# Row factors of three norms sent to all partitions through a DRAM scratch instead of through TensorE

## Chip, cores and metric

The kernel runs on one core of a Trainium2 chip. The metric is the device time of one execution in microseconds, as the median of several; lower is better.

## What is computed

A sequence of 256 tokens with 1024 features passes through four residual blocks, and nearly all of the work is matrix products in fp32 quality. Cut to what matters here:

```python
def rmsnorm(x, g):                                   # also rms_norm of the second part
    y = x * lax.rsqrt(jnp.mean(x * x, axis=-1, keepdims=True) + 1e-6)
    return y * g

# first part, two layers
h = h + attention(rmsnorm(h, norm_mix[0]))           # norm L0
h = h + sq_relu_mlp(rmsnorm(h, norm_mlp[0]))         # norm M0
h = h + rglru_block(rmsnorm(h, norm_mix[1]))         # norm L1
h = h + sq_relu_mlp(rmsnorm(h, norm_mlp[1]))         # norm M1
h = rmsnorm(h, norm_final)
# second part, one layer
h = h + 0.5 * swiglu(rms_norm(h, ffn1_norm), gate, up, down)   # norm F1
h = h + mixer(rms_norm(h, mix_norm))                           # norm X2
h = h + 0.5 * swiglu(rms_norm(h, ffn2_norm), gate, up, down)   # norm F2
out = rms_norm(h, final_norm)

def swiglu(x, w_gate, w_up, w_down):
    return (jax.nn.silu(x @ w_gate) * (x @ w_up)) @ w_down
```

A norm divides each token (row) by a factor of its own. That division commutes with a product over the features, so the kernel multiplies the un-normed rows by the weights and applies the factor afterwards.

## The kernel before, in words

**Pieces.** All weights stream through SBUF as 167 pieces of 1 MB, each of 128 partitions by 2048 fp32. SyncE loads a piece into one of four `raw` buffers as soon as `lo_done` says that an earlier one is free. ScalarE (`hi`) rounds it to `w_hi`, VectorE (`lo`) subtracts to get `w_lo`, and TensorE multiplies with both halves, so that three products stand for one fp32 product. ScalarE and VectorE stay three pieces ahead of TensorE (`LOOK`). Every engine runs its own program in written order, and semaphores tie them together.

**A SwiGLU block** (`feed_forward` for `F1` and `F2`) goes over 11 pairs of column blocks. For each pair TensorE multiplies a gate piece and an up piece (`u_piece` with `u_wide`), and a down piece of the pair before (`d_piece`). The results of the up products have the features on the partitions and the tokens along the free axis. So the row factor, which is one number per token, is needed as a row of 256 numbers that is the same on all 128 partitions: the tile `rms`. For pair 0 VectorE runs `gate` (times `rms`), ScalarE the Silu, then VectorE and ScalarE make `z`, `z_hi` and `z_lo` (`z_finish`), and the first `d_piece` of TensorE waits for both (`z_ready`). The sums `tmp[0]` and `tmp[1]` have left PSUM before that, so nothing but this chain needs `rms`.

**The attention block** (`L0`) needs `rms` when `qk_leave` copies the query and key products out of PSUM. Its position bias is made on GpSimd's queue: a table goes to a DRAM scratch (`er_dram`), comes back by a 2 MB transfer into `bias`, and a memset closes it (`bias_done`).

**How `rms` is made before.** The factors exist as `rstd`, with a token on each partition (128 partitions by 2). GpSimd computes it in `rstds` (a power of -0.5). VectorE's `diags(j)` multiplies the identity by each of the two columns. TensorE's `spread(j)` multiplies a matrix of ones by the two diagonals into a PSUM bank, and VectorE's `spread(j)` copies that bank into `rms`. This stands at five norms (`SPREAD`: L0, L1, F1, X2, F2). At F1 the factor is the product of two norms' factors: `both_rstds()` multiplies `rstd` by `rstd2` on VectorE after the split of piece `n0 + 4` and signals `rstd_both`. TensorE's `spread(F1)` comes after product 7 of the second gate piece, and `spread(F2)` after product 4 of its own; `spread(L0)` stands right ahead of the query and key pieces.

**GpSimd's queue** also issues the small constant loads: after `hn_rstd` of F1 the rope table, `mats`, the mask and `pool_m`; after `rstds(F2)` the last norm's gain.

## Time and profile before

| | |
|---|---|
| median of 3 runs | 1013.86 us (1012.96 to 1013.97) |
| the profiled execution | 1013.26 us |
| its span, first to last instruction | 1011.5 us |
| TensorE busy | 1003.2 us, 99% |
| VectorE, ScalarE, GpSimd busy | 68%, 55%, 3% |
| granted TensorE clock, mean | 0.999 |
| HBM read and written | 183.14 MB and 1.07 MB |

The time of an execution is 1.8 us more than its span, and the profiled execution lies 0.6 us below the median. Busy times of TensorE are modelled for a pipelined engine, so that what a matmul costs is the distance from its start to the next start, and not its own duration.

### The profile page before, as it was taken

What the parts mean: (1) busy time and instruction counts of PE and PEld (TensorE: products, weight loads), DVE (VectorE), ACT (ScalarE), POOL (GpSimd) and SP (SyncE); (2) the same over time, 40 slices, a digit from 0 to 9 for tenths busy, and PEclk for the clock granted to TensorE, in tenths of its full rate; (3) what the DMA queues carried; (4) which work ended last, traced back from release to release, by engine and by line L of the source; (5) the groups of instructions that cost most, each with busy time, mean ns of one, the idle gap of its engine ahead of it and who ended that gap; (6) DMA issues with size and microseconds to landing.
All of it is one profiled execution on the core that took longest, in us unless ns stands there. A gap on an engine that the chain in (4) does not pass through costs nothing.

```text
span 1011.5 us, 14177 instructions
## 1 busy us (share of the span) xinstructions
PE 1003.2 (99%) x5632; PEld 857.4 (85%) x5632; DVE 684.5 (68%) x925; ACT 556.8 (55%) x807; POOL 35.0 (3%) x38
## 2 busy tenths in 40 slices
PE   9999999999999999999999999999999999999997
PEld 7988788888889988888888888888888788888886
DVE  6777676666667887666566766656578767666564
ACT  6678654444456866443444645545457655545453
POOL 1000010000002300000000200000010010000000
PEclk9999999999999999999999999999999999999999
DMA  9943385564553445745655566565633365665621
GB/s 339 324 133 126 125 280 176 200 208 167 188 187 126 167 167 193 245 167 199 212 173 171 207 198 226 190 208 167 208 114 107 115 204 172 228 208 167 208 84 42
DMA packets 122287, 185.13 MB, mean 183 GB/s; under 512 B 3130, under 2 KB 100590, under 8 KB 122094
## 3 DMA queue, kind: packets, MB, share of 16 engines
q1 hardware_dynamic: 119952, 176.70, 52.4%
q0 software_dynamic: 1808, 6.93, 1.9%
q8 instruction: 45, 0.74, 0.3%
q10 hardware_dynamic: 462, 0.60, 0.2%
q14 instruction: 20, 0.16, 0.0%
HBM read 183.14 MB, written 1.07 MB: 182 GB/s over the span
## 4 chain that ended last, share of the span: by engine, by line
PE 96%; DVE 2%; ACT 1%; DMA 1%; issue 1%; SPq 0%
PE bank L1493 37%; PE bank L1470 28%; PE bank L1472 14%; PE bank L1456 3%; PE bank L1458 3%; PE bank L1459 3%; PE bank L1519 1%; DVE w_lo L784 1%; PE bank L1614 1%; PE bank L1665 1%; PE bank L1642 1%; PE bank L1626 1%; DMA raw<-in_w_qkv 1%; PE bank L1810 0%; PE bank L1811 0%
## 5 line engine op out<-in xcount | busy, mean ns | idle before, releaser
L784 DVE TENSOR_TENSOR w_lo<-raw,w_hi 128x2048 fp32r<-128x2048 f32 x164 | 374.0, 2289 | 130.5 <-ACT w_hi L386 130.5
L1470 PE MATMUL bank<-xT,w_hi 128*128 128x512 f32 x1216 | 431.4, 398 | 0.0
L1472 PE MATMUL bank<-xT,w_lo 128*128 128x256 f32 x1216 | 341.1, 280 | 0.0
L386 ACT ACTIVATE w_hi<-raw 128x2048 fp32r<-128x2048 f32 x164 | 311.7, 1908 | 37.5 <-PE bank L1493 33.5
L1470 PEld LDWEIGHTS bank<-xT,w_hi 128*128 128x128 f32 x1216 | 228.4, 188 | 55.7 <-issue 0.3
L1472 PEld LDWEIGHTS bank<-xT,w_lo 128*128 128x128 f32 x1216 | 229.6, 189 | 1.9
L1493 PE MATMUL bank<-w_hi,z_hi 128*128 128x512 f32 x472 | 153.9, 394 | 0.2
L1493 PE MATMUL bank<-w_lo,z_hi 128*128 128x512 f32 x472 | 152.3, 391 | 0.0
L1493 PE MATMUL bank<-w_hi,z_lo 128*128 128x512 f32 x472 | 151.7, 390 | 0.0
L429 ACT ACTIVATE work<-bank 128x256 f32<-128x256 f32 x152 | 49.8, 379 | 178.8 <-PE bank L1472 178.8
L859 DVE TENSOR_TENSOR work<-bank,work 128x256 f32<-128x256 f32 x152 | 57.1, 418 | 74.0 <-ACT work L429 74.0
L1493 PEld LDWEIGHTS bank<-w_lo,z_hi 128*128 128x128 f32 x472 | 88.6, 188 | 19.3 <-issue 0.2
L1493 PEld LDWEIGHTS bank<-w_hi,z_lo 128*128 128x128 f32 x472 | 88.6, 188 | 19.3
L1493 PEld LDWEIGHTS bank<-w_hi,z_hi 128*128 128x128 f32 x472 | 85.0, 188 | 18.5 <-issue 1.3
L1456 PE MATMUL bank<-xT,w_hi 128*128 128x256 f32 x304 | 89.9, 296 | 0.0
L444 ACT ACTIVATE z_hi<-work 128x512 fp32r<-128x512 f32 x54 | 34.1, 632 | 99.7 <-DVE work L876 53.0
L1458 PE MATMUL bank<-xT,w_hi 128*128 128x256 f32 x304 | 85.9, 282 | 0.0
L1459 PE MATMUL bank<-xT,w_lo 128*128 128x256 f32 x304 | 85.8, 282 | 0.0
L887 DVE TENSOR_TENSOR z_lo<-work,z_hi 128x512 fp32r<-128x512 f32 x54 | 37.4, 692 | 37.7 <-ACT z_hi L444 37.7
L1456 PEld LDWEIGHTS bank<-xT,w_hi 128*128 128x128 f32 x304 | 58.0, 191 | 2.4 <-issue 1.2
L1458 PEld LDWEIGHTS bank<-xT,w_hi 128*128 128x128 f32 x304 | 58.1, 191 | 0.3
L1459 PEld LDWEIGHTS bank<-xT,w_lo 128*128 128x128 f32 x304 | 58.1, 191 | 0.0
(215 smaller groups left out, 775.5 us busy)
## 6 DMA issues: line engine op xcount, KB each, us to landing
raw<-in_w SPq DMA_DIRECT2D x64, 1024.0 KB, 5.3
raw<-in_f_gate SPq DMA_DIRECT2D x22, 1024.0 KB, 5.3
raw<-in_f_up SPq DMA_DIRECT2D x22, 1024.0 KB, 5.8
raw<-in_f_down SPq DMA_DIRECT2D x22, 1024.0 KB, 4.9
raw<-in_w_in SPq DMA_DIRECT2D x13, 1024.0 KB, 5.4
raw<-in_w_qkv SPq DMA_DIRECT2D x9, 1024.0 KB, 8.6
raw<-in_w_o SPq DMA_DIRECT2D x4, 1024.0 KB, 5.0
raw<-in_rec_w_o SPq DMA_DIRECT2D x4, 1024.0 KB, 5.2
```

Of the source, the lines that this page charges most:

```text
L386: e.activation(w_hi[n % RING], raw[n % RAW], ACT.Copy).then_inc(hi_done, 1)
L429: e.activation(low[:, b * S:(b + 1) * S], bank[n][:, S:2 * S], ACT.Copy).then_inc(z_low, 1)
L444: e.activation(z_hi[:, s, :], tmp[f.nu], ACT.Copy).then_inc(zhi_done, 1)
L784: e.tensor_tensor(w_lo[n % RING], raw[n % RAW], r32(w_hi[n % RING]), ALU.subtract).then_inc(lo_done, 1)
L859: e.tensor_tensor(t[:, here], bank[n][:, 0:S], low[:, here], ALU.add).then_inc(z_sum, 1)
L887: e.tensor_tensor(z_lo[:, s, :], z, r32(z_hi[:, s, :]), ALU.subtract).then_inc(zlo_done, 1)
L1456: e.matmul(o, whi[:, k, cut], xT_hi[:, k, :], start=(k == 0 and b == 0), stop=False, skip_group_check=True)
L1458: e.matmul(o, whi[:, k, cut], xT_lo[:, k, :], start=False, stop=False, skip_group_check=True)
L1459: last = e.matmul(o, wlo[:, k, cut], xT_hi[:, k, :], start=False, stop=(k == KB - 1), skip_group_check=True)
L1470: e.matmul(bank[i], whi[:, k, cut], xT[:, k, :, :].rearrange("p b s -> p (b s)"), start=(k == 0), stop=False, skip_group_check=True)
L1472: last = e.matmul(bank[i][:, 0:S], wlo[:, k, cut], xT_hi[:, k, :], start=False, stop=(k == KB - 1), skip_group_check=True)
L1493: mm = e.matmul(acc[t][half], x, w[:, kk, half * 512:(half + 1) * 512], start=(first and kk == 0 and x is xhi and w is whi), stop=(last an ...
```

## The change

`SPREAD` now holds only L1 and X2. At L0, F1 and F2 the diagonals, the matmuls by ones and the copy from PSUM are gone. In their place GpSimd writes `rstd` to a DRAM scratch `rms_dram` as a row of 256 numbers (`factors_out`), waits until that has landed, and reads the row back into `rms` on all 128 partitions (`factors_in`). What used to wait for `rms_done` at these norms now waits for `rms_in`.

```diff
-SPREAD = {j: i + 1 for i, j in enumerate((L0, L1, F1, X2, F2))}
+NORMED = {j: i + 1 for i, j in enumerate((L0, L1, F1, X2, F2))}
+SPREAD = {L1: 1, X2: 2}
...
@@ vector(e) @@
         def diags(j):
-            if j == F1:
-                e.wait_ge(rstd_both, 1)
-            else:
-                e.wait_ge(rstd_done, SPREAD[j])
+            e.wait_ge(rstd_done, NORMED[j])
...
-            if j in SPREAD and j != F1:
+            if j in SPREAD:
                 diags(j)
...
@@ gate(f, p) @@
             else:
-                e.wait_ge(rms_done, SPREAD[f.j])
+                e.wait_ge(rms_in[f.j], 16)
             e.tensor_tensor(pair(tmp[0]), pair(tmp[0]), rms_pair(), ALU.mult).then_inc(z_g, 1)
...
                 if f.j == F1:
                     both_rstds()
-                    diags(F1)
...
-                spread(f.j)
+                if f.j == F1:
+                    e.wait_ge(rstd_both, 1)
+                else:
+                    e.wait_ge(rstd_done, NORMED[f.j])
                 e.tensor_scalar(down_scale, rstd, 0.5, None, ALU.mult).then_inc(scale_done, 1)
                 gate(f, 0)
...
         variance(L0)
-        diags(L0)
...
         lo(5)
-        spread(L0)
         lo(6)
-        e.wait_ge(rms_done, SPREAD[L0])
+        e.wait_ge(rms_in[L0], 16)
         qk_leave(0)
...
@@ gpsimd(e) @@
+        def factors_out(j):
+            e.dma_start(rms_dram[NORMED[j] - 1, :].rearrange("(t p) -> p t", p=P), rstd,
+                        allow_slow_non_contiguous=True).then_inc(rms_out[j], 16)
+
+        def factors_in(j):
+            e.wait_ge(rms_out[j], 16)
+            e.dma_start(rms, row_bcast(rms_dram[NORMED[j] - 1, :], S)).then_inc(rms_in[j], 16)
...
         rstds(L0)
+        e.wait_ge(rstd_done, NORMED[L0])
+        factors_out(L0)
+        factors_in(L0)
         e.wait_ge(er_out, 16)
         e.dma_start(bias, bass.AP(tensor=er_dram.tensor, offset=0, ap=[[1, P], [ER, N_HEADS], [1, S]])).then_inc(
             in_bias, 16)
...
         e.tensor_tensor(rstd2, var, minus_half, ALU.pow).then_inc(hn_rstd, 1)
+        e.wait_ge(rstd_both, 1)
+        factors_out(F1)
+        factors_in(F1)
         e.dma_start(cs_t, A["rope"]).then_inc(in_rope, 16)
...
         rstds(F2)
+        e.wait_ge(rstd_done, NORMED[F2])
+        factors_out(F2)
+        factors_in(F2)
         e.dma_start(nf, row_bcast(A["norm_last"], D)).then_inc(in_norm_last, 16)
...
@@ tensor(e) @@
-                ups(p, {7 if f.j == F1 else 4: lambda: spread(f.j)} if p == 1 and f.nu == 2 else None)
+                ups(p)
...
-        spread(L0)
...
-        e.wait_ge(rms_done, SPREAD[L0])
         e.wait_ge(bias_done, 1)
```

Line numbers of the changed kernel run higher than those of before: `w_lo` of a piece is L784 before and L787 now, a matmul of the up products L1470 and L1472 before and L1487 and L1489 now, one of the down products L1493 and L1510.

On GpSimd, at the attention norm L0, the queue stood so before; the first row is the factor, `work<-er_scratch` is the 2 MB load of the bias, and the memset closes the bias.

```order
L1397 DMA er_scratch<-work 16x384 [waits er_far,er_near]
L1385 TENSOR_TENSOR rstd<-var,minus_half 128x2 [waits var_done,consts]
L1401 DMA work<-er_scratch 128x16x256 [waits er_out]
L1404 MEMSET work 64x16x64 [waits in_bias]
L1406 DMA gate_w<-in_w_ga 128x8x128 [waits var_done]
```

Now it stands so.

```order
L1405 DMA er_scratch<-work 16x384 [waits er_far,er_near]
L1385 TENSOR_TENSOR rstd<-var,minus_half 128x2 [waits var_done,consts]
L1388 DMA rms_scratch<-rstd 128x2x1 [waits rstd_done]
L1393 DMA rms<-rms_scratch 128x256 [waits rms_out0]
L1412 DMA work<-er_scratch 128x16x256 [waits er_out]
L1415 MEMSET work 64x16x64 [waits in_bias]
```

Two transfers have moved in ahead of the bias load, and the second of them waits for the landing of the first.

On GpSimd at F1 and F2 the queue now reads as follows; without the four rows that name `rms_scratch` it is the order of before.

```order
L1446 TENSOR_TENSOR rstd<-var,minus_half 128x2 [waits hn_var]
L1388 DMA rms_scratch<-rstd 128x2x1 [waits rstd_both]
L1393 DMA rms<-rms_scratch 128x256 [waits rms_out4]
L1450 DMA work<-in_rope 128x512
L1451 DMA work<-in_mats 128x640
L1452 DMA work<-in_mask 128x512
L1453 DMA work<-in_pool_m 128x2048
L1385 TENSOR_TENSOR rstd<-var,minus_half 128x2 [waits var_done] x2
L1388 DMA rms_scratch<-rstd 128x2x1 [waits rstd_done]
L1393 DMA rms<-rms_scratch 128x256 [waits rms_out6]
L1459 DMA work<-in_norm_last 128x1024
```

The constant loads of F1 now stand behind the pair of transfers, and so does the gain of the last norm.

On VectorE at F1 the rows from the product of the two factors to the first `z_lo` were these before.

```order
L784 TENSOR_TENSOR w_lo<-raw,w_hi 128x2048 [waits hi_done,z_sum]
L905 TENSOR_TENSOR rstd<-rstd 128x2 [waits hn_done,hn_rstd]
L828 TENSOR_SCALAR diag<-ident,rstd 128x128 [waits rstd_both]
L828 TENSOR_SCALAR diag<-ident,rstd 128x128
L851 COPY rms<-bank 128x256 [waits spread_done]
L928 TENSOR_SCALAR down_scale<-rstd 128x2
L867 TENSOR_TENSOR work<-work,rms 128x512 [waits rms_done]
L884 TENSOR_TENSOR work<-work 128x512 [waits z_s]
L887 TENSOR_TENSOR z_lo<-work,z_hi 128x512 [waits z_f,zhi_done]
```

Now they are these.

```order
L787 TENSOR_TENSOR w_lo<-raw,w_hi 128x2048 [waits hi_done,z_sum]
L905 TENSOR_TENSOR rstd<-rstd 128x2 [waits hn_done,hn_rstd]
L930 TENSOR_SCALAR down_scale<-rstd 128x2 [waits rstd_both]
L867 TENSOR_TENSOR work<-work,rms 128x512 [waits rms_in4]
L884 TENSOR_TENSOR work<-work 128x512 [waits z_s]
L887 TENSOR_TENSOR z_lo<-work,z_hi 128x512 [waits z_f,zhi_done]
L787 TENSOR_TENSOR w_lo<-raw,w_hi 128x2048 [waits hi_done]
```

Three rows are gone, and the multiplication by `rms` (L867) waits for the second transfer in place of the copy.

## Rows read from the trace of the kernel before

**Rows 1.** The page: busy time, share of the span and instructions of each engine.

```profile
PE 1003.2 (99%) x5632; PEld 857.4 (85%) x5632; DVE 684.5 (68%) x925; ACT 556.8 (55%) x807; POOL 35.0 (3%) x38
```

**Rows 2.** The page: the chain that ended last, share of the span by engine.

```profile
PE 96%; DVE 2%; ACT 1%; DMA 1%; issue 1%; SPq 0%
```

**Rows 3.** Waits of TensorE: engine line waited for: us in total, times, longest.

```profile
PE bank L1650 <- POOL zeros L1387: 1.0, 1, 1.0
PE bank L1626 <- DVE work L990: 0.9, 2, 0.5
PE bank L1665 <- ACT w_hi L391: 0.2, 1, 0.2
...
PEld bank L1614 <- DVE z_lo L951: 0.4, 1, 0.4
```

**Rows 4.** One line, the matmuls by ones: count, ns min/median/max, first and last start.

```profile
L1561 PE MATMUL bank<-diag,ones x20: 270/275/377, 30.2 to 835.8; 128*128 128x128 f32 x20
```

**Rows 5.** TensorE in order of time at F1: start us, us, what.

```profile
576.77 0.67 PE L1561 MATMUL bank<-diag,ones 128*128 128x128 f32 x4
577.20 0.47 PE L1470 MATMUL bank<-xT,w_hi 128*128 128x512 f32 x1
577.51 0.27 PE L1472 MATMUL bank<-xT,w_lo 128*128 128x256 f32 x1
...
582.48 0.40 PE L1470 MATMUL bank<-xT,w_hi 128*128 128x512 f32 x1
582.71 0.28 PE L1472 MATMUL bank<-xT,w_lo 128*128 128x256 f32 x1
582.83 0.62 PE L1493 MATMUL bank<-w_hi,z_hi 128*128 128x512 f32 x2
```

**Rows 6.** VectorE in order of time at F1.

```profile
576.20 0.15 DVE L905 TENSOR_TENSOR rstd<-rstd 128x2 f32<-128x2 f32 x1
...
577.94 0.69 DVE L867 TENSOR_TENSOR work<-work,rms 128x512 f32<-128x512 f32 x1
...
580.72 0.69 DVE L887 TENSOR_TENSOR z_lo<-work,z_hi 128x512 fp32r<-128x512 f32 x1 [0.70 <-ACT z_hi L444]
```

**Rows 7.** DMA issues of the whole span: KB each, median us to landing.

```profile
er_scratch<-work POOLq DMA_DIRECT2D x1, 24.0 KB, 5.5
work<-in_norm_final POOLq DMA_DIRECT2D x1, 512.0 KB, 3.7
work<-in_norm_last POOLq DMA_DIRECT2D x1, 512.0 KB, 6.1
work<-in_rel POOLq DMA_DIRECT2D x1, 16.1 KB, 4.5
out<-work SPq DMA_DIRECT2D x2, 256.0 KB, 2.0
raw<-in_w_qkv SPq DMA_DIRECT2D x9, 1024.0 KB, 8.6
```

**Rows 8.** GpSimd in order of time at L0 and at F2.

```profile
23.21 1.22 POOL L1401 DMA_DIRECT2D work<-er_scratch  x1
35.22 0.95 POOL L1404 MEMSET work<- 64x1024 f32 x1 [10.79 <-DMA work<-er_scratch]
...
827.42 0.58 POOL L1442 DMA_DIRECT2D work<-in_norm_last  x1
```

**Rows 9.** VectorE in order of time at L0, what `rms` and the bias release.

```profile
38.59 0.68 DVE L1042 SCALAR_TENSOR_TENSOR work<-bank,rms 128x512 f32<-128x512 f32 x1
...
43.69 0.76 DVE L951 TENSOR_TENSOR z_lo<-work,z_hi 128x256 fp32r<-128x256 f32 x2 [0.59 <-ACT z_hi L483]
```

**Rows 10.** VectorE and TensorE in order of time at F2.

```profile
837.36 0.69 DVE L867 TENSOR_TENSOR work<-work,rms 128x512 f32<-128x512 f32 x1
...
843.54 0.62 PE L1493 MATMUL bank<-w_hi,z_hi 128*128 128x512 f32 x2
```

**Rows 11.** TensorE at the start, and one down piece in the chain.

```profile
0.99 3.60 PE L1650 MATMUL bank<-zeros 128*128 128x128 bf16 x32 [0.99 <-POOL zeros L1387]
...
503.08 5.46 PE bank L1493 x24
```

**Rows 12.** Cores: span and mean granted TensorE clock.

```profile
core 0: 1011.5 us, clock 0.999
```

More of the change, by code:

```diff
@@ L186, in build @@
     x_first = sem("x_first")
+    rms_out, rms_in = ({j: sem(f"rms_{k}{j}") for j in NORMED if j not in SPREAD} for k in ("out", "in"))
     ss_both, var_done, rstd_done, diag_done, spread_done, rms_done = (sem(n) for n in (
@@ L254, in build @@
     MIX_BANK = {0: 0, 1: 2, 4: 0}
-    spread_bank = {L0: bank[7], L1: bank[7], F1: bank[1], X2: bank[7], F2: bank[1]}
+    spread_bank = {L1: bank[7], X2: bank[7]}
     a_ = vec("a_param")
@@ L265, in build @@
     qT, kT, bias = at(24, KB, S), at(32, KB, S), at(8, N_HEADS, S)
+    rms_dram = nc.dram_tensor("rms_scratch", [len(NORMED), S], F32, kind="Internal").ap()
     er_dram = nc.dram_tensor("er_scratch", [N_HEADS, ER], F32, kind="Internal").ap()
@@ L556, in scalar @@
             e.wait_ge(v_closed, t + 1)
-            e.wait_ge(rstd_done, SPREAD[L0])
+            e.wait_ge(rstd_done, NORMED[L0])
             for half in range(2):
@@ L725, in scalar @@
             scale_weights(a2, 0, hd)
-        e.wait_ge(rstd_done, SPREAD[X2])
+        e.wait_ge(rstd_done, NORMED[X2])
         pc_leave(0)
@@ L892, in normed_h @@
             e.wait_ge(turned, KB * F1 + KB)
-            e.wait_ge(rstd_done, SPREAD[F1])
+            e.wait_ge(rstd_done, NORMED[F1])
             for t in range(T):
@@ L1399, in gpsimd @@
         rstds(L0)
+        e.wait_ge(rstd_done, NORMED[L0])
+        factors_out(L0)
+        factors_in(L0)
         e.wait_ge(er_out, 16)
@@ L1564, in feed_forward, with ups @@
         def feed_forward(f, j_next):
-            def ups(p, between=None):
+            def ups(p):
                 for i in range(f.nu):
@@ L1570, in ups @@
                         e.wait_ge(z_sum, 2 * f.sums(before, i))
-                    u_piece(f.ups(p) + i, f.banks(p, i), between if i == 0 else None, u_wide)
+                    u_piece(f.ups(p) + i, f.banks(p, i), None, u_wide)
             def z_ready(p):
```

## The prediction

> **What bounds the kernel now.** I read the busy times of the engines first, then the chain of work that ended last, then the waits of TensorE, and last the timelines of the engines around each of the three norms. TensorE is busy for 99% of the span and the next engine, VectorE, for 68% [rows 1]. The chain that ended last runs through TensorE for 96% of the span [rows 2]. TensorE's own waits are three kinds that sum to about 2 us, none longer than 1.0 us, and one of its weight loads waits 0.4 us for a `z_lo` of the attention [rows 3]. So whatever is taken out of TensorE's program shortens the kernel, and whatever makes TensorE stand still lengthens it by as much. Nothing later can take such a stall back, since there is no idle time on TensorE to absorb it. Work on VectorE or GpSimd counts only where TensorE waits for its end.
>
> **What the change takes out.** The matmuls by ones appear as 20 records for five norms, so four a norm, of 275 ns each [rows 4]. That would be 1.1 us a norm and 3.3 us in all, but the records overlap. What counts is the distance between starts [rows 5]: at F1 the four begin at 576.77 and the next product at 577.20, which is 0.43 us; the product behind them takes 0.31 us to the following start (577.20 to 577.51), where an undisturbed one takes 0.23 us (582.48 to 582.71), so another 0.08 us. One spread costs TensorE 0.5 us, and three cost 1.5 us. That is what can be gained. The six diagonals and three copies on VectorE are gone as well; I cost them at nothing, because VectorE is the engine that waits at these places, and at F1 the copy's place is taken by a wait.
>
> **What the change puts in at F1.** The product of the factors ends at 576.35 (576.20 and 0.15) [rows 6]. Before, the multiplication by `rms` started at 577.94, so that the whole way over diagonals, TensorE and the copy took 1.6 us. From that start to the end of the first `z_lo` (580.72 and 0.69, so 581.41) are 3.47 us [rows 6]: the multiplication, the Silu, the product, the rounding, the subtraction, each waiting for the one before. TensorE started its first down product, which needs that `z_lo`, at 582.83 [rows 5]. Without the spread it would be there at 582.33. So the slack was 1.4 us, and with the matmuls gone it is 0.9 us. Now two transfers in series take the place of the 1.6 us. Let R be the time from the product of the factors to the landing of the second. Then `z_lo` ends at 576.35 + R + 3.47, and TensorE stands still for 576.35 + R + 3.47 − 582.33 = R − 2.5 us. It stops paying to remove the matmuls as soon as R − 2.5 is over 1.5, so at R = 4.0 us.
>
> Behind the waiting multiplication VectorE has the split of the next piece queued, and ScalarE the Silu, the rounding of `z` and its own split. They move by the same amount, but TensorE's down piece takes 5.46 us [rows 11] and all of them follow within it, as they do now, so nothing further is late and the stall is paid once. The product of the factors itself is no later than before, as it waits for nothing new.
>
> **What R is.** The trace has no transfer of 4-byte elements and no row read back on all partitions from a scratch. The nearest rows [rows 7]: the write of the bias table to its scratch, from the same queue, took 5.5 us from issue to landing for 24 KB, in a stretch crowded with weight loads; a 16 KB load on this queue took 4.5 us; gains broadcast to all partitions took 3.7 and 6.1 us for 512 KB. The lower bound of one transfer is the 2.0 us of the output stores at the end, from SyncE's queue with nothing beside them; the upper is the 6.1 us. The write out is 256 elements of four bytes, small but in many parts, and a 1 MB weight load is issued at about the same moment; I take it nearer to the two small transfers than to the stores, 4.3 us. The read back is 128 KB, a quarter of the gain's, and may meet the tail of that load; I take 3.6 us, just under the faster gain. Two wake-ups of about 0.1 us each make R = 8.1 us, with ends at 4.2 (twice 2.0 and 0.2) and 11.8 (5.5, 6.1 and 0.2). The stall is then 5.6 us, with ends at 1.7 and 9.3.
>
> The Trainium skill gives a DMA from GpSimd's path about 2.0 us fixed plus its bytes over 436 GB/s ("DMA: Bandwidth & Descriptors", section "Anatomy of one DMA — SWDGE (gpsimd) path"). By that, as an estimate, R would be 4.5 us, the stall 2.0 us and the net 0.5 us slower. The rows speak against it: no transfer of this queue landed in under 3.7 us, a 16 KB one not in under 4.5 us.
>
> **F2.** The factor was ready when the gain's load was issued, at 827.42 [rows 8]. The multiplication by `rms` started at 837.36 and the first down product at 843.54 [rows 10]. TensorE would be there at 843.04 now, so `rms` must be in by 843.04 − 3.47 = 839.57, which allows R up to 12.1 us. Even the upper end of R fits. I cost it at nothing; the cover is the two gate and up pieces between factor and first down piece, which here follow a factor that was ready 9.9 us before its use. At F1 the factor comes only 1.6 us before its use, since the second norm's squares stand between.
>
> **L0.** The factor is ready by 23.21, when the bias load was issued [rows 8]. `rms` is first used at 38.59 [rows 9], 15.4 us later, so even R = 11.8 is covered. What moves is the bias: its load now waits for the first transfer's landing and for the issue of the second. With 5.5 us for the write, as the table's was in the same crowded stretch, and about 0.6 us for an issue (0.58 [rows 8]), it starts 6.2 us later, and its memset ends at 42.4 in place of 36.17. VectorE's first instruction behind `bias_done` started at 43.69 [rows 9]. That leaves 1.3 us, so I cost it at nothing, but it is thin: a write that takes over 6.8 us makes TensorE wait, since its scores already wait 0.4 us for that `z_lo` [rows 3]. The four constant loads behind F1's pair and the gain behind F2's are used long afterwards.
>
> **Sum.** Minus 1.5 us for three spreads, plus 5.6 us at F1, is plus 4.1 us. The profiled execution had 1013.26 us (a span of 1011.5 and 1.8 around it), so 1017.4 by its own time; the median of the runs lies 0.6 us above it, and I forecast 1018.0 us.
>
> **The rivals.**
> - *The clock falls in the stall (slower still).* TensorE's mean granted clock is 0.999 [rows 12], and it is never idle for more than 1.0 us [rows 3], so the trace cannot show what a stall of 5 us does. If the clock falls to 1.2 GHz, the down piece after it starts slowly. The price lies between nothing and a whole down piece at half speed, another 5.46 us [rows 11]. The nearest row is the start of the program, where 32 matmuls of 128 columns out of idleness took 3.60 us, 112 ns each; in the down piece 512 columns take 5.46/24 = 227 ns, which is 57 ns for 128. If such a stretch follows the stall, half of its 3.6 us is lost, 1.8 us, and the time is 1019.8. Against it: the profile's granted clock is not lower at the start either. The Trainium skill has this as a rule ("TensorE: Matmul & The Clock Gate", section "The HAM clock gate"): an idle stretch takes TensorE back to half rate.
> - *The transfers are quick (no change).* If both land like the stores at the end, R = 4.2, the stall is 1.7 us, the net plus 0.2, and the time 1014.1. For it speaks that both are small and that the constant loads, which shared the DMA engines before, now come afterwards; against it, that no transfer of this queue did so well.
> - *Quicker than before.* R below 3.0 us would make the kernel over 1 us faster, at best 1012.4 with R under 2.5. It decides at R = 4.0 us, so one transfer in 1.9 us. No row comes near it.
> - *The bias is late as well (slower still).* If the write at L0 takes 8.6 us, as the median of the query and key pieces did there [rows 7], the bias closes 9.3 us later, at 45.5, which is 1.8 us behind the use. TensorE stalls in the scores, and the time is 1019.8, or up to 1023 with the high end of R at F1.
>
> **How the numbers follow.** The stall at F1 alone has 0.42, with its own range of 1015.9 to 1021.7 (R from 6.0 to 11.8). The fall of the clock has 0.26, the late bias 0.12, the quick transfers 0.17 and quicker than before 0.03. The range is 1014.6 to 1022.5: below it lie the fastest case and most of the quick one, above it only the slow ends of two. About 0.2%, 2.0 us, is what a measurement of this kernel can tell from no change. Faster by more than that has 0.03, within it 0.17 (R under about 6), and slower 0.80.
>
> **What would show it.** TensorE should show one new wait, of its first down product at F1 for `z_lo` L887, of 3 to 9 us, and VectorE's L867 should wait for the DMA into `rms` by about as much more as the slack. At F2 L867 should not wait for it. The records of ones times diagonals should be 8. At L0 the bias memset should end before 43.7. The step I trust least is R. If L867 at F1 starts before 581, the stall is small and the forecast too high; if the granted clock reads lower behind the stall, the second case holds; if a wait of the scores at L0 for `z_lo` grows, the bias is late.

## The result and the profile after

| | before | changed |
|---|---|---|
| median | 1013.72 us (4 runs, 1012.96 to 1013.97) | 1045.01 us (4 runs, 1041.34 to 1046.18) |
| the profiled execution, its span | 1013.26, 1011.5 us | 1044.58, 1042.8 us |
| mean granted clock | 0.999 | 0.985 |

The changed kernel takes 1.0303 times as long, with a 95% interval of 1.0288 to 1.0318. The forecast was 1018.0 us with a range up to 1022.5, so the sign was right and the size far off: 31.3 us more and not 4.1. Everything below is read from one profiled execution of each kernel, unless a median is named.

The page of the changed kernel, its busy times and the chain by engine and line:

```profile
PE 1009.1 (97%) x5620; PEld 861.3 (83%) x5620; DVE 682.0 (65%) x916; ACT 558.0 (54%) x807; POOL 38.9 (4%) x44
...
PE 86%; DMA 6%; DVE 3%; ACT 2%; issue 1%; SPq 1%; POOL 0%; DVEq 0%; POOLq 0%
PE bank L1510 35%; PE bank L1487 25%; PE bank L1489 13%; DMA rms_scratch<-rstd 3%; PE bank L1473 3%; PE bank L1475 3%; PE bank L1476 3%; DMA work<-er_scratch 1%; DMA rms<-rms_scratch 1%; DMA raw<-in_w_qkv 1%; PE bank L1631 1%; DVE w_lo L787 1%; PE bank L1536 1%; PE bank L1659 1%; PE bank L1643 1%
```

TensorE's share of the chain fell from 96% [rows 2] to 86%, and a write of 1 KB, `rms_scratch<-rstd`, now holds 3% of it. TensorE executes 12 matmuls fewer, the twelve by ones, and has three new waits of over 1 us. Its waits, and behind them those of VectorE and GpSimd that feed them (us in total, times, longest):

```profile
PE bank L1510 <- ACT z_hi L447: 17.6, 2, 13.4
PE bank L1631 <- DVE z_lo L953: 7.0, 1, 7.0
```

```profile
POOL rms L1393 <- DMA rms_scratch<-rstd: 29.0, 3, 10.3
DVE work L867 <- DMA rms<-rms_scratch: 22.8, 2, 15.7
DVE z_lo L953 <- POOL work L1415: 7.4, 1, 7.4
```

Those are stalls of 13.4 us at F1, 4.2 us at F2 (17.6 less 13.4) and 7.0 us at L0, where the forecast had one of 5.6. The DMA issues tell why (KB each, median us to landing; the first two were not in the trace of before, the last three answer to [rows 7] and [rows 8]):

```profile
rms_scratch<-rstd POOLq DMA_DIRECT2D x3, 1.0 KB, 10.2
rms<-rms_scratch POOLq DMA_DIRECT2D x3, 128.0 KB, 5.8
raw<-in_w_qkv SPq DMA_DIRECT2D x9, 1024.0 KB, 11.9
er_scratch<-work POOLq DMA_DIRECT2D x1, 24.0 KB, 5.4
work<-er_scratch POOLq DMA_DIRECT2D x1, 2048.0 KB, 14.8
```

The smallest transfer of the program is the slowest of the small ones. In the same crowded stretch the table's write of 24 KB still takes 5.4 us, as it did before. At F1 the pair stands so on GpSimd, and its result so on VectorE and TensorE (start us, us, what, in brackets the idle time and its releaser):

```profile
586.36 0.77 POOL L1388 DMA_DIRECT2D rms_scratch<-rstd  x1 [3.96 <-DVE rstd L905]
596.15 0.56 POOL L1393 DMA_DIRECT2D rms<-rms_scratch  x1 [9.02 <-DMA rms_scratch<-rstd]
...
602.01 0.69 DVE L867 TENSOR_TENSOR work<-work,rms 128x512 f32<-128x512 f32 x1 [15.74 <-DMA rms<-rms_scratch]
...
605.58 1.19 PE L1510 MATMUL bank<-w_hi,z_hi 128*128 128x512 f32 x2 [13.39 <-ACT z_hi L447]
...
613.88 0.39 PE L1487 MATMUL bank<-xT,w_hi 128*128 128x512 f32 x1
```

The write takes 9.8 us and the read back 5.9. Behind the stall the down piece runs from 605.58 to 613.88, 8.30 us, where it took 5.46 [rows 11]. The windows around it (us, busy and count of PE, PEld, DVE, ACT, POOL, then granted clock, DMA share, GB/s) show the clock at half, its 1.2 GHz level, from the stall into the piece:

```profile
594.00:596.00 2.00, 0.00 (x0) 0.00 (x0) 0.00 (x0) 0.00 (x0) 0.00 (x0) 0.59 0.00 0
596.00:610.00 14.00, 4.42 (x11) 3.49 (x12) 5.46 (x7) 3.61 (x5) 2.67 (x5) 0.50 0.54 146
610.00:612.00 2.00, 2.00 (x7) 1.61 (x6) 0.27 (x1) 1.70 (x2) 0.00 (x0) 0.65 0.85 252
```

GpSimd's DMA queue shows the write's own packets between 590 and 592:

```profile
q0 software_dynamic: 32, 0.00, 1.5%
```

The last of them ends at 591.1, and from there to 596 the DMA engines move nothing at all while the write is still out. So it is not short of bandwidth, and the DMA engines are not busy with its parts either: 5 of the 9.8 us pass between the end of the last packet and the landing. Another 3.9 pass before the first packet, at 590.3, while a weight load runs.

At L0 `rms` was late as well, which TensorE's waits don't show:

```profile
40.29 0.69 DVE L1044 SCALAR_TENSOR_TENSOR work<-bank,rms 128x512 f32<-128x512 f32 x1 [2.60 <-DMA rms<-rms_scratch]
```

VectorE waited 2.6 us for it. This cost TensorE nothing of its own, since the bias, which the scores need next, came later still.

**The account.** GpSimd computes one factor at each of the norms L0, L1, F1, X2 and F2, and its starts cut the span into stretches. I use them for every run below (us, start of the span to L1's factor, then from factor to factor, the last to the end of the span; L0's transfers lie in the first stretch, F1's in the third, F2's in the last).

| | to L1 | L1 to F1 | F1 to X2 | X2 to F2 | F2 to end |
|---|---|---|---|---|---|
| before | 306.40 | 257.19 | 186.76 | 74.45 | 186.70 |
| changed | 316.10 | 257.19 | 202.59 | 74.47 | 192.45 |
| difference | +9.70 | 0.00 | +15.83 | +0.02 | +5.75 |

The differences sum to 31.3 us. A stretch without a removed spread keeps its time to 0.02 us. In each of the other three the stall less the spread's 0.5 us leaves a rest: 9.7 = 7.0 − 0.5 + 3.2 at L0, 15.8 = 13.4 − 0.5 + 2.9 at F1, 5.75 = 4.25 − 0.5 + 2.0 at F2. The lowered clock accounts for nearly all of it. At F1 the down piece took 8.30 − 5.46 = 2.84 us more, and at F2 it took 7.16 (873.19 to 880.35), 1.7 more; the other 0.3 us there stay open. At L0 the granted clock was half (0.50 to 58, 0.89 from 58 to 60) for 6.5 us after TensorE went on at 51.96, and half of 6.5 is 3.2.

### The profile page after: what moved, and what is told of

Same layout as the page of the kernel before. It is cut to its first block, busy times and chain, and to the rows that moved or that the text cites. A ratio compares the mean times of both kernels' runs of the same rounds, so it can differ in the third digit from the quotient of the medians.

```text
span 1042.8 us, 14149 instructions
## 1 busy us (share of the span) xinstructions
PE 1009.1 (97%) x5620; PEld 861.3 (83%) x5620; DVE 682.0 (65%) x916; ACT 558.0 (54%) x807; POOL 38.9 (4%) x44
## 4 chain that ended last, share of the span: by engine, by line
PE 86%; DMA 6%; DVE 3%; ACT 2%; issue 1%; SPq 1%; POOL 0%; DVEq 0%; POOLq 0%
PE bank L1510 35%; PE bank L1487 25%; PE bank L1489 13%; DMA rms_scratch<-rstd 3%; PE bank L1473 3%; PE bank L1475 3%; PE bank L1476 3%; DMA work<-er_scratch 1%; DMA rms<-rms_scratch 1%; DMA raw<-in_w_qkv 1%; PE bank L1631 1%; DVE w_lo L787 1%; PE bank L1536 1%; PE bank L1659 1%; PE bank L1643 1%
## 5 line engine op out<-in xcount | busy, mean ns | idle before, releaser
L787 DVE TENSOR_TENSOR w_lo<-raw,w_hi 128x2048 fp32r<-128x2048 f32 x164 | 374.0, 2290 | 132.7 <-ACT w_hi L389 132.7
L1487 PE MATMUL bank<-xT,w_hi 128*128 128x512 f32 x1216 | 431.4, 398 | 0.0
L1489 PE MATMUL bank<-xT,w_lo 128*128 128x256 f32 x1216 | 341.1, 281 | 0.0
L1487 PEld LDWEIGHTS bank<-xT,w_hi 128*128 128x128 f32 x1216 | 228.4, 188 | 56.0 <-issue 0.3
L1489 PEld LDWEIGHTS bank<-xT,w_lo 128*128 128x128 f32 x1216 | 229.6, 189 | 1.9
L1510 PE MATMUL bank<-w_hi,z_hi 128*128 128x512 f32 x472 | 155.8, 398 | 17.7 <-ACT z_hi L447 17.6
L1510 PE MATMUL bank<-w_lo,z_hi 128*128 128x512 f32 x472 | 153.6, 394 | 0.0
L1510 PE MATMUL bank<-w_hi,z_lo 128*128 128x512 f32 x472 | 153.4, 393 | 0.0
L1510 PEld LDWEIGHTS bank<-w_hi,z_hi 128*128 128x128 f32 x472 | 86.3, 191 | 36.9 <-ACT z_hi L447 18.2
L1510 PEld LDWEIGHTS bank<-w_lo,z_hi 128*128 128x128 f32 x472 | 89.5, 190 | 19.7 <-issue 0.2
L1510 PEld LDWEIGHTS bank<-w_hi,z_lo 128*128 128x128 f32 x472 | 89.5, 190 | 19.6
## 6 DMA issues: line engine op xcount, KB each, us to landing
raw<-in_w_qkv SPq DMA_DIRECT2D x9, 1024.0 KB, 11.9
```

Source lines behind the costliest of these rows:

```text
L787: e.tensor_tensor(w_lo[n % RING], raw[n % RAW], r32(w_hi[n % RING]), ALU.subtract).then_inc(lo_done, 1)
L1487: e.matmul(bank[i], whi[:, k, cut], xT[:, k, :, :].rearrange("p b s -> p (b s)"), start=(k == 0), stop=False, skip_group_check=True)
L1489: last = e.matmul(bank[i][:, 0:S], wlo[:, k, cut], xT_hi[:, k, :], start=False, stop=(k == KB - 1), skip_group_check=True)
L1510: mm = e.matmul(acc[t][half], x, w[:, kk, half * 512:(half + 1) * 512], start=(first and kk == 0 and x is xhi and w is whi), stop=(last an ...
```

## The experiments

**1. What the small write costs by itself.** A kernel of its own, which does nothing but such transfers one after the other, first idle, at the end beside a stream of 1 MB loads.

```python
"el": lambda e: e.dma_start(ap(d_el, [1, P], [P, T]), fac, ...),              # 256 of 4 B, neighbours, as in the change
"pt": lambda e: e.dma_start(ap(d_pt, [T, P], [1, T]), fac),                   # 128 runs of 8 B, neighbours
"half": lambda e: e.dma_start(ap(d_half, [1, P], [1, 1]), fac[:, 0:1], ...),  # 128 of 4 B, neighbours
"far": lambda e: e.dma_start(ap(d_far, [16, P], [16 * P, T]), fac, ...),      # 256 of 4 B, 64 B apart
"rows": lambda e: e.dma_start(ap(d_rows, [P, T], [1, P]), row[0:T, 0:P]),     # 2 rows of 512 B
"back": lambda e: e.dma_start(back, ap(d_rows, [0, P], [1, S])),              # the read back to 128 partitions
```

The comments are mine, and `...` stands for a flag. `d_page` has its parts 4 KB apart, `d_sp` is `d_el` from SyncE's queue, and `d_bel`, `d_bpt` and `d_brows` are `d_el`, `d_pt` and `d_rows` beside the stream.

> This kernel computes nothing of the reference (the output is zeros); it times single transfers, each waited for, three times each. On an idle core from GpSimd's queue: 256 elements of 4 bytes from [128,2] to a row (d_el), the same in 128 runs of 8 bytes (d_pt), 128 elements of 4 bytes (d_half), 256 elements set 64 bytes (d_far) and 4 KB apart (d_page), two runs of 512 bytes (d_rows), 128 runs of 1 KB (d_big), the read back on all partitions (back), 4-byte reads (few); the 4-byte write from SyncE's queue (d_sp); then d_bel, d_bpt and d_brows beside a stream of weight loads. Theory A, the number of 4-byte parts is what costs: d_el about 9.5 us, alone and beside the stream, d_half and d_pt about 5 to 6, d_far and d_page as d_el, d_rows 2.5, d_sp about 9. Theory B, the stream of weights is what delays it: d_el under 4 us, d_bel about 10. Theory C, GpSimd's software queue is slow: d_sp under 4 us with d_el about 9.5 and d_rows slow too. Theory D, the writes fall into one short piece of DRAM and stand in each other's way: d_el about 9.5, d_far and d_page under 5.

Measured (4 KB apart took 2.0 as well), as the DMA issues of that kernel (KB each, median us to landing):

```profile
d_el<-fac POOLq DMA_DIRECT2D x3, 1.0 KB, 8.3
d_pt<-fac POOLq DMA_DIRECT2D x3, 1.0 KB, 3.4
d_half<-fac POOLq DMA_DIRECT2D x3, 0.5 KB, 7.8
d_far<-fac POOLq DMA_DIRECT2D x3, 1.0 KB, 2.0
d_rows<-row POOLq DMA_DIRECT2D x3, 1.0 KB, 1.5
d_sp<-fac SPq DMA_DIRECT2D x3, 1.0 KB, 8.9
d_bel<-fac POOLq DMA_DIRECT2D x3, 1.0 KB, 11.9
```

The read back takes 3.3 us. The write takes 8.3 us with nothing beside it (the median of three issues, which lay 8.1 to 10.2 us before the next; 11.9 beside the stream), so traffic is not its main cost. The number of parts isn't either: the same 256 parts at 64 bytes take 2.0 us, and half as many neighbours take 7.8. SyncE's queue is no quicker, so it isn't GpSimd's. What is left is that the parts are neighbours in DRAM. A read doesn't suffer from it: 256 neighbouring 4-byte parts were read from DRAM (`few`) in 2.5 us. Beside the stream the runs of 8 bytes lost most of their advantage, 9.5 us (`d_bpt`) in place of 3.4, while the two rows took 5.3 (`d_brows`).

The time does not pass in the DMA engines. The first write of neighbours is issued at 3.38 us and landed when the next is issued at 11.49; of its windows (us, busy of GpSimd, granted clock, DMA share, GB/s) only the first has packets:

```profile
4.70:5.10 0.40, 0.00 (x0) 1.00 0.12 3
5.10:11.40 6.30, 0.00 (x0) 1.00 0.00 0
```

The write at 64 bytes, issued at 65.06, shows the same 32 packets and the same share of 0.12 in the 0.4 us from 66.30 on, and the next issue follows at 67.31. Both keep the DMA engines busy alike; what differs is the time from the last packet to the landing.

**2. How near is near.** The same kind of kernel with the distance varied, and the same small parts sent into SBUF.

```python
def strided(t, k):      # 256 of 4 B, 4*k bytes apart
    return lambda e: e.dma_start(ap(t, [k, P], [k * P, T]), fac, allow_slow_non_contiguous=True)
...
    "el": strided(d_el, 1), "s8": strided(d_s8, 2), "s16": strided(d_s16, 4), "s32": strided(d_s32, 8),
    "s64": strided(d_s64, 16),
...
    "lined": lambda e: e.dma_start(lined[0:1, 0:P], fac[:, 0:1], ...),   # 128 of 4 B, neighbours in one SBUF partition
    "bel": strided(d_bel, 1), "bfar": strided(d_bfar, 16),               # beside the stream
```

> Again single transfers, nothing of the reference computed (the output is zeros), three times each: the write of 256 elements of 4 bytes with neighbours 4 bytes (d_el), 8 (d_s8), 16 (d_s16), 32 (d_s32) and 64 bytes (d_s64) apart in DRAM, two runs of 512 bytes (d_rows), 128 elements of 4 bytes into one partition of SBUF (lined); beside a stream of weight loads d_bel, d_bfar (64 bytes apart), lined_b, and the read back on all partitions (back_b). Theory D (writes of fewer bytes than a piece of DRAM of fixed size stand in each other's way when they fall into the same piece): the time falls with the distance, about 8.3, 5, 3, 2.3 and 2.0 us, with the step where each element has a piece to itself; d_bfar 4 to 6, as two runs had beside the stream; lined about 2 since SBUF is no DRAM. Rival, that neighbouring addresses must be adjacent to be merged (any gap helps): d_s8 is already at 2.0. Beside the stream the read back takes 5 to 6 us, as in the changed kernel.

GpSimd's timeline of that kernel; each issue waits for the landing before it, so the distance of two starts is one write. The three writes from 30.57 on have parts 8 bytes apart, the three from 41.76 on 16, those from 48.91 on 32, the last three 64; `d_rows` follows:

```profile
30.57 0.73 POOL L40 DMA_DIRECT2D d_s<-fac  x1 [7.73 <-DMA d_el<-fac]
34.30 0.72 POOL L40 DMA_DIRECT2D d_s<-fac  x1 [3.00 <-DMA d_s<-fac]
...
41.76 0.72 POOL L40 DMA_DIRECT2D d_s<-fac  x1 [3.01 <-DMA d_s<-fac]
44.02 0.72 POOL L40 DMA_DIRECT2D d_s<-fac  x1 [1.54 <-DMA d_s<-fac]
...
48.91 0.72 POOL L40 DMA_DIRECT2D d_s<-fac  x1 [1.55 <-DMA d_s<-fac]
...
60.18 0.73 POOL L40 DMA_DIRECT2D d_s<-fac  x1 [1.54 <-DMA d_s<-fac]
62.43 0.53 POOL L45 DMA_DIRECT2D d_rows<-row  x1 [1.52 <-DMA d_s<-fac]
```

| distance in DRAM, bytes | 4 | 8 | 16 | 32 | 64 |
|---|---|---|---|---|---|
| one write, idle, from issue to the next issue, us | 8.2 to 10.5 | 3.7 | 2.3 to 2.6 | 2.25 | 2.25 |

128 neighbours in SBUF (`lined`) cost 1.9 us, where 128 in DRAM took 7.8. Beside the stream the read back took 6.1 us, the 64-byte write 4.8 (its first of three 8.7 to the next issue) and the neighbours 11.0 (medians of three). So the idle write's time falls as the distance grows from 4 to 16 bytes and is nearly flat from there on, and that belongs to the DRAM end. The rival that any gap is enough fails at 8 bytes, which took 3.7 us and not 2. What happens in the memory I infer only: the parts that fall into one short piece of DRAM seem to wait for each other. No run looks into the memory.

The Trainium skill ("DMA: Bandwidth & Descriptors", section "Specifications") says that a transfer under 512 bytes is written by read-modify-write. That can be the mechanism by which neighbours wait for each other, which no run here shows. Size alone does not decide: all columns of the table have parts of 4 bytes, eight of them fall into 512 bytes at the largest distance, and that one takes 2.0 us by its own landing.

**3. The losses one by one.** F1 goes by diagonals and ones again; L0 and F2 stay changed.

```diff
-SPREAD = {L1: 1, X2: 2}
+SPREAD = {L1: 1, F1: 2, X2: 3}
...
-        e.wait_ge(rstd_both, 1)
-        factors_out(F1)
-        factors_in(F1)
```

> F1 gets its factors by diagonals again; L0 and F2 keep the DRAM way. The trace of the changed kernel puts 15.8 us of the loss between the norms F1 and X2. If the three losses are independent: 1045.0 - 15.8 = 1029.2 us, within 1.5. If lateness carried from L0 is part of it (or the loads moved behind the pair at F1 cost something later), it stays above 1032.

Measured 1028.51 us (1026.28 to 1029.51), 1.0139 times before [1.0122, 1.0157]. The stretches are 313.14, 257.15, 186.85, 74.45 and 194.31: F1 is back at its old time. F2 lost 7.6 us with a stall of 5.2, where it had lost 5.75. L0 lost 6.7 us and not 9.7: the stall was 2.7 us, since the bias load took 12.1 (35.16 to 47.28) and not 14.8. The total is that of the expectation, so F1's loss doesn't depend on the other two. The losses at L0 and F2 differ by 2 to 3 us between the two executions, and why the transfers take longer in one than in the other isn't shown.

**4. Is it the wait that delays the bias at L0?** The 2 MB bias load is issued ahead of the two small transfers.

```diff
-        factors_out(L0)
-        factors_in(L0)
         e.dma_start(bias, ...er_dram...)
+        factors_out(L0)
+        factors_in(L0)
         e.wait_ge(in_bias, 16)
```

> At L0 the 2 MB bias load is issued ahead of the two small transfers; all else as in the changed kernel. Theory: L0's loss of 9.7 us is the bias, pushed back by the first transfer's landing. Then the stall of the scores nearly vanishes; rms comes about 1 us later than before needed, so up to 1.5 us stay: 1035.3 to 1037. Rival: it is the late rms that holds L0 up; then the time stays at 1043 to 1047.

Measured 1045.02 us (1044.31 to 1045.25), 1.0304 times before [1.0288, 1.0319]: nothing gained. My expectation missed, and the rival's number held. GpSimd and VectorE at L0:

```profile
24.66 0.73 POOL L1388 DMA_DIRECT2D rms_scratch<-rstd  x1
41.04 0.60 POOL L1393 DMA_DIRECT2D rms<-rms_scratch  x1 [15.65 <-DMA rms_scratch<-rstd]
41.63 0.97 POOL L1415 MEMSET work<- 64x1024 f32 x1
...
48.15 0.69 DVE L1044 SCALAR_TENSOR_TENSOR work<-bank,rms 128x512 f32<-128x512 f32 x1 [10.36 <-DMA rms<-rms_scratch]
```

The bias is in time now, the memset at 41.63 (the slack ends at 43.69 [rows 9]). But the small write shares the DMA engines with 2 MB more and takes 16.4 us, and `rms` comes 9.6 us after its use at 38.59 [rows 9]. TensorE's wait for the attention's `z_lo` is 8.0 us. With the write ahead of the bias load `rms` was late as well, but by 1.7 us (40.29 after 38.59), hidden behind the later bias. The order decides which of the two is late by enough to stop TensorE.

**5. The transfers alone, without the rest of the change.** The kernel before, with both transfers of L0 added into a spare tile ahead of the bias load. The diagonals and ones stay.

```diff
+        e.wait_ge(rstd_done, SPREAD[L0])
+        e.dma_start(rms_dram.rearrange("(t p) -> p t", p=P), rstd, ...).then_inc(rms_out, 16)
+        e.wait_ge(rms_out, 16)
+        e.dma_start(spare, row_bcast(rms_dram, S)).then_inc(rms_in, 16)
         e.wait_ge(er_out, 16)
```

> The kernel before, diagonals everywhere, with one thing added: at L0 GpSimd also does the 4-byte write to a scratch, waits for it, and reads it back into a spare tile that nobody uses, all ahead of the bias load. Theory: L0's loss is the bias behind the first transfer, so this alone costs L0's whole loss of 9.7 us and the 0.4 us of the matmuls that are still there: 1013.6 + 10.1 = 1023.7 us (1021 to 1026). Rival, that L0 waits for rms: 1013 to 1015.

Measured 1020.53 us (1018.49 to 1021.46), 1.006 times before [1.0043, 1.0077]. A pair of transfers that nobody reads costs 7 us, since the bias stands behind it. I had expected 1021 to 1026, so it is a little less than the whole loss at L0. TensorE's new wait and what precedes it on GpSimd:

```profile
PE bank L1621 <- DVE z_lo L953: 5.5, 1, 5.5
```

```profile
23.89 0.77 POOL L1403 DMA_DIRECT2D rms_scratch<-rstd  x1 [0.29 <-POOL rstd L1387]
...
49.27 0.94 POOL L1411 MEMSET work<- 64x1024 f32 x1 [12.52 <-DMA work<-er_scratch]
```

The first stretch takes 314.89, 8.5 us more than before, and all others keep their time. The stall accounts for 5.5 of it; the rest, 3.0, is about what the lowered clock took at L0 in the changed kernel. There the stretch lost 10.2 us if the saved spread is left out (9.7 and 0.5), with a stall 1.5 us longer. Nobody waits for the read back here, so the late bias is enough to make the loss.

**6. The clock in F1's stall.** TensorE gets 200 small matmuls of zeros into an unused bank ahead of the wait, which takes nothing from the wait itself.

```diff
+FILL = 200
...
                 ups(p)
+                if p == 1 and f.j == F1:
+                    for _ in range(FILL):
+                        e.matmul(bank[0][:, 0:P], zeros, zeros, start=True, stop=True)
                 z_ready(p - 1)
```

> TensorE does 200 matmuls of zeros into an unused bank ahead of its wait at F1, which change no result. Theory: the down piece after the stall took 8.3 in place of 5.46 us since the clock had fallen; kept busy, TensorE stays at 2.4 GHz and the time is 1045.0 - 2.8 = 1042.2 us, with the granted clock at 1.00 around F1. Rival: the slow piece is due to something else, such as the delayed constant loads: no change, 1045.

Measured 1040.69 us (1040.47 to 1041.56), 1.0264 times before [1.0247, 1.0281], 4.3 us under the changed kernel. TensorE's timeline and the windows:

```profile
591.27 11.34 PE L1602 MATMUL bank<-zeros 128*128 128x128 bf16 x200
604.28 0.70 PE L1511 MATMUL bank<-w_hi,z_hi 128*128 128x512 f32 x2 [1.66 <-ACT z_hi L448]
```

```profile
590.00:604.00 14.00, 12.61 (x209) 12.16 (x207) 1.90 (x3) 1.81 (x3) 2.67 (x5) 1.00 0.46 134
604.00:610.00 6.00, 5.72 (x25) 4.79 (x26) 3.83 (x5) 2.79 (x5) 0.00 (x0) 1.00 0.25 75
```

The clock stays at 1.00, its 2.4 GHz level, and the down piece takes 5.54 us (604.28 to 609.82) in place of 8.30. F1's stretch is 199.31, 3.3 us less; 2.8 of these are the clock, and the other 0.5 an earlier `rms`. The other 1.0 us of the 4.3 was gained elsewhere, mostly in L0's stretch (0.7 us less, with a stall of 6.3 in place of 7.0), where nothing was edited. So the fall of the clock in an idle stretch is a loss of its own, on top of the stall, and work on TensorE prevents it.

**7. The write made quick.** The factors are written 64 bytes apart at all three norms, and `rms` is read back from a contiguous row of an input, so that it holds other numbers and this kernel leaves the true factors out.

```diff
-            e.dma_start(rms_dram[NORMED[j] - 1, :].rearrange("(t p) -> p t", p=P), rstd,
+            far = bass.AP(tensor=rms_dram.tensor, offset=(NORMED[j] - 1) * S * 16, ap=[[16, P], [16 * P, T]])
+            e.dma_start(far, rstd,
...
-            e.dma_start(rms, row_bcast(rms_dram[NORMED[j] - 1, :], S))
+            e.dma_start(rms, row_bcast(A["norm_final"], S))
```

> The changed kernel with the 256 elements written 64 bytes apart, and the read back taken from a contiguous row of an input once that write has landed: the same transfers, waits and order, but rms holds other numbers, so this leaves the true factors out. Theory: the write lands in 2 to 5 us in place of 10. At F1 R is about 9, the stall 6.5, the slow clock 2.8, less the 1.4 saved: 1013.6 + 7.9 = 1021.5 us (1018.5 to 1023.5); L0 and F2 no longer stall. Rival, that the write is slow in the kernel for its number of parts or its neighbours in the queues: 1040 to 1045.

Measured 1023.07 us (1022.7 to 1023.87), 1.0093 times before [1.0078, 1.0108]: of 31 us lost 22 come back, as expected (1018.5 to 1023.5). Of the three new waits of TensorE one is left, 8.3 us at F1, and the two transfers there are these:

```profile
576.44 0.77 POOL L1389 DMA_DIRECT2D rms_scratch<-rstd  x1 [3.96 <-DVE rstd L905]
582.53 0.56 POOL L1394 DMA_DIRECT2D rms<-in_norm_final  x1 [5.33 <-DMA rms_scratch<-rstd]
```

Beside the weights even this write takes 6.1 us, and the read 4.5 us, a little quicker than from the scratch (5.8), which is a second difference of this run. The stretches are 306.17, 257.20, 197.38, 74.42 and 186.33: L0 and F2 no longer lose and gain 0.2 and 0.4 us; F1 loses 10.6, that is 8.3 − 0.5 and 2.8 for the clock.

**8. The change at its best places.** Quick writes at L0 and F2 as in the run before, again with `rms` from the input and the true factors left out, and F1 by diagonals.

> The factors of F1 go by diagonals and ones again, as before the change; at L0 and F2 they are written to DRAM 64 bytes apart, and rms is read back from a contiguous row of an input (so the true factors of L0 and F2 are left out of rms). This is the change at its best places with a quick write. If the adjacent writes are the whole loss at L0 and F2, TensorE has no wait over 1 us and two spreads of 0.5 us are saved: 1012.6 us, between 1011.8 and 1013.4, so under 0.2% off the kernel before. Rival: moving the bias load, or the transfers beside the weights, costs TensorE something of its own even when the write is quick: 1014 to 1017 us.

Measured 1011.89 us (11 runs, 1011.45 to 1012.91), beside 1012.69 for the kernel before on the same chip, 0.9987 times [0.9978, 0.9997]. TensorE has no wait over 1.1 us. The gain is 0.8 us (0.3 to 2.2 by the interval), which fits the 1.0 that two spreads cost. That is all there was to win at these two norms.

**9. A whole version of it.** The factors lie 16 bytes apart, and the whole 4 KB are read back to each partition, from which VectorE takes every fourth number.

```diff
+            apart = bass.AP(tensor=rms_dram.tensor, offset=(NORMED[j] - 1) * S * 4, ap=[[4, P], [4 * P, T]])
+            e.dma_start(apart, rstd, ...)
...
+            e.dma_start(rms_wide[j], row_bcast(rms_dram[NORMED[j] - 1, :], S * 4)).then_inc(rms_in[j], 16)
...
+            return bcast(rms_wide[j], [0, 2], [4, S])
```

> A whole version of the one before: F1 by diagonals, and at L0 and F2 each factor is written to DRAM 16 bytes from the next (the gaps are filled once at the start), the row of 4 KB is read back as it stands to all partitions (512 KB), and VectorE reads every fourth number of it. Idle, writes at 16 bytes took 2.3 to 2.6 us. If that holds up beside the weights (under 6.8 us at L0, as the 6.1 us of the 64-byte ones) and the four times larger read back does not delay the bias by more than the rest of the slack, the time is that of the last run relative to before, 0.8 us less, give or take 0.4. Rival: the write beside the weights, or the larger read ahead of the bias at L0, makes the bias late: 1 to 5 us more than before, with a wait of the scores for z_lo. At F2 both theories expect no wait (R under 12.1 us).

Measured 1016.19 us (10 runs, 1014.69 to 1016.96) beside 1013.75 for the kernel before, 1.0019 times [1.001, 1.0029]: 2.4 us slower. That is the number of the rival, but not its mechanism. GpSimd at L0, and VectorE's first multiplication by `rms`:

```profile
24.35 0.77 POOL L1399 DMA_DIRECT2D rms_scratch<-rstd  x1 [0.29 <-POOL rstd L1395]
30.54 0.57 POOL L1404 DMA_DIRECT2D work<-rms_scratch  x1 [5.42 <-DMA rms_scratch<-rstd]
...
43.64 0.95 POOL L1430 MEMSET work<- 64x1024 f32 x1 [11.36 <-DMA work<-er_scratch]
...
38.27 1.10 DVE L1054 SCALAR_TENSOR_TENSOR work<-bank,work 128x512 f32<-128x512 f32 x1
```

The write landed in 6.2 us, as quick as at 64 bytes in run 7. The larger read in front of the bias load makes the memset end at 44.6, 0.9 us past the slack, but L0's factor started 0.8 us later in this execution (23.34 after 22.53), and the scores never waited: TensorE has no wait for a `z_lo`. Its longest new wait is for VectorE's copy of L1002, 1.4 us at 62.59 where the same wait was 0.5 us before, and behind it the granted clock fell:

```profile
PE bank L1655 <- DVE work L1002: 2.4, 4, 1.4
...
64.00:80.00 16.00, 16.00 (x125) 14.59 (x126) 11.98 (x33) 9.86 (x29) 0.00 (x0) 0.89 0.22 74
```

The first stretch takes 309.92, 3.5 us more. The later start is 0.8 of it, the waits of L1655 are 1.5 more than before, the clock at half for 3.4 us (64.6 to 68.0) costs 1.7, and the spread saves 0.5. On VectorE each multiplication by the spread-out row takes 1.10 us in place of 0.68 [rows 9]; that this makes the wait is likely, but not shown. F2's stretch is 186.38, 0.3 us less than before. So a version with F2 alone would gain 0.3 us, which no measurement here could tell from nothing, and I did not run it.

## Why the prediction was wrong

- **What bounds the kernel: right.** Every us of TensorE's stalls is in the time; the stretches show nothing taken back later.
- **What is taken out, 0.5 us a norm: right in size.** The run at its best places gained 0.8 us (0.3 to 2.2) where 1.0 was forecast for two norms.
- **R at F1: the step that failed.** The prediction took 4.3 us for the write and 3.6 for the read back, 8.1 with the wake-ups. They were 9.8 and 5.9, and R was 15.9 (15.65 from 586.36 to 602.01, and 0.3 from the product's end at 586.06 to the issue). The upper bound of the write, 5.5 us, came from the write of the table, 24 KB in rows that are contiguous in DRAM; that row was still right for what it is (5.4 us after the change). It was no bound for 256 neighbouring parts of 4 bytes, since none of the rows had a part that small. The sentence "small but in many parts" named the difference and then priced it at nothing. Idle, the same write takes 8.3 us, over its upper bound already. The lower values that the prediction weighed, an R of 4.2 and of 4.5 us, were further off still.
- **The stall as R − 2.5: right.** With R = 15.9 it gives 13.4 us, and 13.4 was measured; run 7 with its 10.9 gives 8.4, measured 8.3.
- **F2 at nothing: wrong by the same term.** Its cover allowed R up to 12.1. `rms` landed 16.3 us after the write was issued (853.30 to 869.62 on the timelines), 4.2 us too late, and the stall is 4.25. The cover itself was worked out rightly; it was tested against an R that was too small.
- **L0 at nothing: wrong by the same term.** The text's limit was a write of 6.8 us. It took 11.0, the bias load behind it 14.8 in place of 12.0, and the stall was 7.0. `rms` itself was said to be covered for an R of 15.4. It came 16.9 us after the factor (23.39 to 40.29), so this cover failed too; the later bias hid it. The rival "the bias is late as well" (0.12) had the place and the mechanism, with a write of 8.6 us and 1.8 us of stall.
- **The clock: the rival held, at all three stalls.** It was estimated at 1.8 us once, with 0.26. It took 2.84 us at F1 and 3.2 and 1.7 us at the two stalls that weren't forecast. Half of a program's start was too small a model: after a 13.4 us stall the first 5.7 us of the down piece ran at half, which is why it took 2.84 us more.
- **The range.** Each rival was weighed with an R from the same rows, so that all of them were short together. The bounds of one unknown term stood under the three steps, and the chances treated these as separate.

With the idle prices of run 1, R is 11.9 us (8.3, 3.3 for the read back, 0.3), and with the loaded ones of run 2 17.4 us (11.0, 6.1, 0.3). That alone would have forecast stalls at F1 of 9.4 to 14.9 us, at L0 in any case (its limit was a write of 6.8), and at F2 for all but the lower end.

## What to carry to other kernels

Before a transfer is priced by a row of the trace, look at how its parts lie in DRAM, their length and their distance, and not at its bytes: a 1 KB write in neighbouring 4-byte parts took 8.3 us alone and about 10 to 16 beside loads, a 24 KB one in long rows 5.4. A column across partitions that must become a row costs that much through DRAM, or 0.5 us of TensorE by diagonals times ones; the second is cheap. If one unknown term stands under several covers, test each against the term's upper end together, and add to a stall of TensorE the clock that it loses behind it, 2 to 3 us here.

## What the runs showed of the hardware

- The time of 4-byte writes to DRAM depends on their distance: idle 8.2 us or more at 4 bytes, 3.7 at 8, 2.3 to 2.6 at 16, 2.25 at 32 and 64. Their number hardly counts (128 took 7.8 us, 256 took 8.3), nor the queue (8.9 from SyncE's), and 128 into SBUF cost 1.9. Idle, the last packet of such a write ends 1.7 us after the issue; the rest is the wait for the landing. Beside a stream, 8-byte neighbours are slow too (9.5 us), and parts 64 bytes apart took 4.8.
- Weight loads beside such a write are late too. The query and key pieces took 8.6 us before [rows 7], 11.9 with the change and 11.6 with the pair added alone (run 5), but 8.8 in run 7, which has the transfers in the same order with the parts 64 bytes apart, and 9.6 in run 9, which reads back from the scratch. So it is the neighbouring parts that slow them, and not the changed order. The bias load took 14.8 us with the change, 9.8 in run 7 and 12.0 before, but 12.1 in run 3, so it varies more.
- At F2 the clock fell with a stall of only 4.25 us, and the windows show it low after TensorE had resumed at 873.19. It also fell 2.1 us into a stall of 2.7 us (48.5, L0 in run 3) and 2.0 us after TensorE had resumed from a wait of 1.4 us (64.6, run 9). In the trace of before, with no wait over 1.0 us, it fell only at 1009.7, after TensorE's last work. The Trainium skill ("TensorE: Matmul & The Clock Gate", section "The HAM clock gate") has the return to half rate out of idleness as a rule; the rows of F2, which follow, agree with it:

```profile
874.00:876.00 2.00, 2.00 (x7) 1.58 (x6) 1.80 (x1) 0.71 (x3) 0.00 (x0) 0.56 0.00 0
876.00:878.00 2.00, 2.00 (x7) 1.56 (x6) 1.85 (x4) 0.08 (x1) 0.00 (x0) 0.59 0.13 20
```
